# Dividing the normalization of the last row tile by columns among VectorE, ScalarE and GpSimd

## The reference

```python
def layer_norm(x, g, b):
    xf = x.astype(jnp.float32)
    mu = jnp.mean(xf, axis=-1, keepdims=True)
    var = jnp.mean(jnp.square(xf - mu), axis=-1, keepdims=True)
    return ((xf - mu) * lax.rsqrt(var + LN_EPS) * g + b).astype(x.dtype)
...
hp = layer_norm(ALPHA * hp + out_p, ln_g[l], ln_b[l])   # 16 meta rows are dropped later, 512 remain
hs = layer_norm(ALPHA * hs + out_s, ln_g[l], ln_b[l])   # 64 rows
```

## Time and profile before

| what | value |
|---|---|
| median of 3 runs | 1019.59 us (1019.33 to 1021.05) |
| the profiled execution's own time | 1020.12 us |
| its span, first to last instruction or landing | 1018.6 us |
| PE busy | 1000.1 us, 98% of the span |
| DVE busy | 715.8 us, 70% |
| ACT busy | 531.7 us, 52% |
| POOL busy | 79.0 us, 8% |
| end of the last matmul in the span | 1008.40 us |
| end of the last DVE instruction | 1015.70 us |

### The profile page before, as it was taken

One profiled execution on the slowest core, in us unless ns is written; L12 is line 12 of the kernel. 1 busy time (PEld: TensorE's weight loads), 2 busy tenths in 40 slices (PEclk: granted clock), 3 DMA queues, 4 the chain that ended last, 5 costly groups with the idle time before them and its releaser, 6 DMA issues.

```text
span 1018.6 us, 20283 instructions
## 1 busy us (share of the span) xinstructions
PE 1000.1 (98%) x7287; PEld 939.8 (92%) x7287; DVE 715.8 (70%) x1423; ACT 531.7 (52%) x1217; POOL 79.0 (8%) x156
## 2 busy tenths in 40 slices
PE   8999999999999999999999999999999999999995
PEld 6989999999999999999999999999999888888884
DVE  6988686876868677686867787767787655141685
ACT  6546455564645555464665776556677662111400
POOL 1520101001010010001010000000000000000000
PEclk9999999999999999999999999999999999999998
DMA  9142333232233313234321222231226543222423
GB/s 349 56 133 95 122 112 127 78 110 98 96 132 110 126 58 108 97 110 140 111 85 65 95 81 97 100 105 52 88 81 237 180 180 104 83 82 82 166 68 118
DMA packets 36258, 115.06 MB, mean 113 GB/s; under 512 B 9312, under 2 KB 9728, under 8 KB 33584
## 3 DMA queue, kind: packets, MB, share of 16 engines
q1 hardware_dynamic: 24208, 87.00, 24.8%
q0 software_dynamic: 11856, 27.14, 7.9%
q10 hardware_dynamic: 144, 0.26, 0.1%
HBM read 99.31 MB, written 18.29 MB: 115 GB/s over the span
## 4 chain that ended last, share of the span: by engine, by line
PE 95%; DMA 2%; DVE 1%; issue 1%; ACT 1%; SPq 0%; DVEq 0%; ACTq 0%
PE ps L1630 33%; PE ps L1640 27%; PE ps L1877 20%; PE ps L1842 5%; PE ps L1816 4%; PE ps L1800 2%; PE ps L1799 2%; DMA w_raw<-in_w_all 1%; PE ps L1862 1%; DMA pt<-in_w_ff 1%; PE ps L1721 1%; PE ps L1820 0%; DVE tb L1283 0%; DVE wl L1106 0%; DVE rows L1607 0%
## 5 line engine op out<-in xcount | busy, mean ns | idle before, releaser
L1630 PE MATMUL ps<-xh,wh 128*128 128x296 f32 (+1 forms) x864 | 261.3, 302 | 2.0 <-DMA pt<-in_w_ff 2.0
L1630 PE MATMUL ps<-xh,wl 128*128 128x296 f32 (+1 forms) x864 | 256.9, 297 | 0.0
L1630 PE MATMUL ps<-xl,wh 128*128 128x296 f32 (+1 forms) x864 | 256.8, 297 | 0.0
L1877 PE MATMUL ps<-wh,mix_parts 128*128 128x512 f32 x576 | 184.2, 390 | 0.0
L1630 PEld LDWEIGHTS ps<-xh,wh 128*128 128x128 f32 x864 | 163.4, 189 | 6.6 <-issue 2.9
L1630 PEld LDWEIGHTS ps<-xl,wh 128*128 128x128 f32 x864 | 163.7, 189 | 0.0
L1630 PEld LDWEIGHTS ps<-xh,wl 128*128 128x128 f32 x864 | 163.2, 189 | 0.0
L1106 DVE TENSOR_TENSOR wl<-w_raw,wh 128x1024 fp32r<-128x1024 f32 (+1 forms) x150 | 143.1, 954 | 19.5 <-ACT wh L841 8.1
L927 ACT ACTIVATE tb<-tb,small 128x256 f32<-128x256 f32 (+5 forms) x160 | 81.3, 508 | 93.4 <-DVE small L1302 64.8
L1877 PEld LDWEIGHTS ps<-wh,mix_parts 128*128 128x128 f32 x576 | 108.1, 188 | 22.4
L1877 PE MATMUL ps<-wl,mix_parts 128*128 128x512 f32 x320 | 124.5, 389 | 0.0
(11 more groups left out here) (196 smaller groups left out, 1732.0 us busy)
## 6 DMA issues: line engine op xcount, KB each, us to landing
w_raw<-in_w_all SPq DMA_DIRECT2D x106, 512.0 KB, 4.3
w_raw<-in_w_all SPq DMA_DIRECT2D x14, 1024.0 KB, 4.8
cbc<-c_rows POOLq DMA_DIRECT2D x16, 360.0 KB, 4.1
x_raw<-in_xT SPq DMA_DIRECT2D x7, 592.0 KB, 12.1
rows<-in_x_p POOLq DMA_DIRECT2D x4, 1024.0 KB, 5.3
out_y_p<-rows SPq DMA_DIRECT2D x16, 256.0 KB, 2.5
mix_rows<-mixT POOLq DMA_DIRECT2D x14, 288.0 KB, 2.4
rel_copies<-rel_rows POOLq DMA_DIRECT2D x8, 384.0 KB, 10.8
```

The source lines that it names most:

```text
L1630: ins = nc.tensor.matmul(ps[:, bank, result(tile, h)], a[f][:, w], b[:, ko, first:first + width], start=(ko == n_first and i == 0), stop=( ...
L1877: ins = nc.tensor.matmul(ps[:, bank, :], a, b[slot][:, w], start=(ko == 0 and i == 0), stop=(ko == KO - 1 and i == len(products) - 1))
```

## The change

Only the last row tile, m = 3, is treated differently. Its four quarters are divided by engine. Quarters 0 and 1 stay on DVE in the two passes of before. Quarter 2 (`mid`) is centred by DVE, scaled by rstd on ACT (`mid_scaled`), and gets its shift added on DVE, with a `tensor_tensor`. Quarter 3 (`end`) is centred and scaled in one ACT instruction, row * rstd + `offset`, where `offset` = -mean * rstd is a new [128, 1] value that DVE computes behind the reciprocal; then POOL multiplies it by gain and adds shift, in two `tensor_tensor` instructions with a wait between them. DVE's order in the last tile becomes: centre quarter 2, reciprocal, offset, centre quarters 0 and 1, scale quarters 0 and 1, add quarter 2's shift. SP stores quarters 0, 1 and 2 on `normed`, and quarter 3, last as before, on the new semaphore `pool_normed`. The other four row tiles keep their order. The diff, without the declarations of `offset` and of the six semaphores:

```diff
-NORM_CUTS = 4
+NORM_CUTS, DVE_CUTS = 4, 2
...
             for i, m in enumerate(last_order):
                 for j in range(NORM_CUTS):
                     c = norm_cut(j)
-                    sp.wait_ge(normed, NORM_CUTS * i + j + 1)
+                    if i == MT - 1 and j == NORM_CUTS - 1:
+                        sp.wait_ge(pool_normed, 1)
+                    else:
+                        sp.wait_ge(normed, NORM_CUTS * i + j + 1)
                     out = y_p[m * P:(m + 1) * P, c] if m < 4 else y_s[:, c]
                     sp.dma_start(out, rows[m][row_range(m), c]).then_inc(y_stored, 16)
             sp.wait_ge(y_stored, NORM_CUTS * 16 * MT)
...
             pool.dma_start(rows[3][:], x_p[3 * P:, :]).then_inc(rows_loaded[3], 16)
             pool.wait_ge(valued, 5 * PAIRS)
             pool.dma_start(rows[4][P - DEC_SEQ:, :], x_s).then_inc(rows_loaded[4], 16)
+            m, end = last_order[-1], norm_cut(NORM_CUTS - 1)
+            pool.wait_ge(norm_loaded, 32)
+            pool.wait_ge(end_scaled, 1)
+            nc.gpsimd.tensor_tensor(rows[m][:, end], rows[m][:, end], gain[:, end], ALU.mult).then_inc(end_gained, 1)
+            pool.wait_ge(end_gained, 1)
+            nc.gpsimd.tensor_tensor(rows[m][:, end], rows[m][:, end], shift[:, end], ALU.add).then_inc(pool_normed, 1)
             for s, n in ((v_stored, KV_SETS), (k_stored, KV_SETS), (kept_stored, 2), (lf_stored, 1)):
                 pool.wait_ge(s, 16 * n)
 
...
                 act.wait_ge(moments_ready, i + 1)
                 nc.scalar.activation(rstd[r, 0, m:m + 1], moments[r, m, 1:2], ACT.Sqrt,
                                      bias=eps[r, :]).then_inc(root_ready, 1)
+            m, mid, end = last_order[-1], norm_cut(DVE_CUTS), norm_cut(NORM_CUTS - 1)
+            act.wait_ge(offset_ready, 1)
+            nc.scalar.activation(rows[m][:, end], rows[m][:, end], ACT.Identity, scale=rstd[:, 1, m:m + 1],
+                                 bias=offset[:]).then_inc(end_scaled, 1)
+            act.wait_ge(mid_centred, 1)
+            nc.scalar.activation(rows[m][:, mid], rows[m][:, mid], ACT.Copy, scale=rstd[:, 1, m:m + 1]
+                                 ).then_inc(mid_scaled, 1)
 
 
 
...
                                   ).then_inc(moments_ready, 1)
                 dve.wait_ge(norm_loaded, 32)
                 dve.wait_ge(moments_ready, i + 1)
-                for j in range(NORM_CUTS):
-                    c = norm_cut(j)
-                    nc.vector.scalar_tensor_tensor(out=rows[m][r, c], in0=rows[m][r, c], scalar=moments[r, m, 0:1],
-                                                   in1=gain[r, c], op0=ALU.subtract,
-                                                   op1=ALU.mult).then_inc(centred, 1)
-                    if j == 0:
+                cuts = range(NORM_CUTS) if i < MT - 1 else range(DVE_CUTS)
+
+                def centre(c):
+                    return nc.vector.scalar_tensor_tensor(out=rows[m][r, c], in0=rows[m][r, c], scalar=moments[r, m, 0:1],
+                                                          in1=gain[r, c], op0=ALU.subtract, op1=ALU.mult)
+
+                if i == MT - 1:
+                    centre(norm_cut(DVE_CUTS)).then_inc(mid_centred, 1)
+                for j in cuts:
+                    if j == (1 if i < MT - 1 else 0):
                         dve.wait_ge(root_ready, i + 1)
                         nc.vector.reciprocal(rstd[r, 1, m:m + 1], rstd[r, 0, m:m + 1]).then_inc(rstd_ready, 1)
+                        if i == MT - 1:
+                            dve.wait_ge(rstd_ready, MT)
+                            nc.vector.scalar_tensor_tensor(out=offset[:], in0=moments[:, m, 0:1], scalar=-1.0,
+                                                           in1=rstd[:, 1, m:m + 1], op0=ALU.mult,
+                                                           op1=ALU.mult).then_inc(offset_ready, 1)
+                    centre(norm_cut(j)).then_inc(centred, 1)
                 dve.wait_ge(rstd_ready, i + 1)
-                for j in range(NORM_CUTS):
+                for j in cuts:
                     c = norm_cut(j)
                     dve.wait_ge(centred, NORM_CUTS * i + j + 1)
                     nc.vector.scalar_tensor_tensor(out=rows[m][r, c], in0=rows[m][r, c], scalar=rstd[r, 1, m:m + 1],
                                                    in1=shift[r, c], op0=ALU.mult, op1=ALU.add).then_inc(normed, 1)
+                if i == MT - 1:
+                    mid = norm_cut(DVE_CUTS)
+                    dve.wait_ge(mid_scaled, 1)
+                    nc.vector.tensor_tensor(rows[m][:, mid], rows[m][:, mid], shift[:, mid], ALU.add).then_inc(normed, 1)
 
 
 
```

More of the change, by code:

```diff
@@ L397, in build @@
         eps = sb("eps", [P, 1], F32, at=norm_at + 640)
+        offset = sb("offset", [P, 1], F32, at=norm_at + 672)
         sample_high = sb("sample_high", [P, 512], F32, at=norm_at + 704)
@@ L470, in build @@
         sample_joined, sample_added = sem("sample_joined"), sem("sample_added")
+        offset_ready, mid_centred, mid_scaled, end_scaled, end_gained, pool_normed = (
+            sem(n) for n in ("offset_ready", "mid_centred", "mid_scaled", "end_scaled", "end_gained", "pool_normed"))
         y_stored = sem("y_stored")
```

## The result

The changed kernel took 1021.81 us (median of 22 runs, 1020.06 to 1022.84), the kernel before 1019.50 us (22 runs, 1018.34 to 1021.29). The ratio is 1.0019 with a 95% interval of 1.0012 to 1.0025: about 1.9 us slower (the medians differ by 2.3). That is just inside the 0.2% that the prediction called no change, though the interval reaches past it, and 0.6 us more than its +1.3.

A forecast was written before the change was run, and what follows sets the result against it. PE bounds all but the tail, which is DVE's chain with transfers close behind; DVE's 1.17 us gain is outweighed by POOL's pair waiting its turn, so 1019.59 + 1.3 = 1020.9 us, range 1018.9 to 1022.0.

The forecast's parts named there:

- What leaves DVE: Tail behind the last matmul: with quarter work moved away, DVE alone ends 1.17 us earlier, at 1014.53.
- What ACT adds: Tail: ACT scales quarter 3 to about 1012.07, then quarter 2 to 1012.78, hidden with 1.06 us to spare.
- Theory B: Set for the follow-ups: new DVE-ACT waits cost the time; without POOL's part still about 1.5 us above, near 1021.
- The port: Tail from 1012.2: a POOL SBUF read and a two-input DVE instruction exclude each other; the loser waits it out.
- the two orders: Handover in the tail: DVE finishes first, +1.35 us, held likelier, or POOL and DVE alternate, +1.56 us.
- the prediction's two witnesses: Early POOL copies: one at 40.56 us waited through two overlapping DVE instructions; the 165-element one got in ahead of one.
- p: Time of one two-input POOL instruction on 128x512 in the tail: taken as 1.2 us, bounds 0.59 and 1.39.
- the in-turn sum: Tail with POOL and DVE instructions alternating: last store issued at 1017.30, landing at 1019.80, +1.56 us.
- rival 1: Tail: POOL runs beside DVE, ending at 1014.75; kernel 0.45 us earlier, 1019.1 us; chance 0.12.
- The signs of being wrong: Tail: POOL's addition ending before 1015.7, DVE waiting for `mid_scaled`, or first store after 1013.4 without POOL ahead.
- Rival 2's load: Before POOL's multiplication: a library's first call, some 6 us, last store near 1023.3, 5 us late; chance 0.02.
- the milder order: Tail: DVE finishes first at 1014.53, then POOL's pair; last store lands at 1019.59, +1.35 us.

The follow-up runs named there:

- the first experiment: The changed kernel with POOL's two instructions moved to DVE, behind quarter 2's last addition, ACT's part kept; 1.0005 (0.9996 to 1.0014) against the kernel before.

## Why the prediction was right, and where its sizes were off

- *What leaves DVE.* Right: 1.17 us. The kernel with shift in PSUM has DVE end 6.11 us behind the last matmul; the prediction's 1014.53 is 6.13 behind 1008.40.
- *What ACT adds.* Right, and hidden: 0.81 us for the scaling with two per-row operands (0.76 was taken), 0.71 for the other. Theory B, that the new waits cost the time, fell with the first experiment.
- *The port.* Right that POOL's reads and DVE's two-input instructions exclude each other: shown by taking the second input away (0.75 us again) and by adding POOL's pair alone (+2.0 us). Of the two orders, the one held to be less likely came: POOL gets in at the handover between two overlapping DVE instructions, each time, in all three kernels in which it meets instructions of two inputs (the changed one and those with POOL's pair and with its smaller one). Of the prediction's two witnesses the 165-element copy went the same way; why the one-element copy at 40.56 us waited through two instructions stays open.
- *p.* The sum took 1.2 us both as POOL's own time and as the time for which it holds DVE up. The hold is 1.0, the bound "two inputs one after the other" of 0.99. As a span in the profile a POOL instruction is longer (1.27 us with no two-input DVE instruction in its way, 1.45 and 1.59 with), so hold and span are two numbers. With 1.0 the in-turn sum puts the last issue at 8.5 us behind the matmul, which is the measured 8.54.
- *The stores.* Missed by 0.4 us: the sum in turn took a landing of 2.5 us. Three stores are issued within 1 us here, and the last lands after 2.9.
- *The end.* Missed by 0.4 us: the sum ended with the landing. POOL's drain was in no term, though its row stood in the trace before, at 841.3 us, 7.18 us long and hidden. Had the port been free (rival 1), the drain would have made that rival's gain a loss, as the kernel with shift in PSUM shows.
- *The signs of being wrong.* Two were set badly. POOL's addition ended at 1015.21, ahead of the 1015.7 that was to show the prediction wrong; but its own sum in turn has that end at 1015.58. And the last store, to be issued at 1017.1 or later, was issued at 1016.76, since p was too long. The first store came at 1014.12, later than 1013.4, with a POOL instruction ahead of it, as the text allowed.
- *Rival 2's load.* The prediction said that the order shows nothing that loads a library for POOL. It passed over the row `ISA` ahead of POOL's first instruction, which the trace has as a pair of MODIFY_POOL_CONFIG at 841.3 us. Whether they load anything is not shown; with 170 us of waiting behind them, their cost would be hidden. The kernel before has such a pair too, at 3.2 and 3.3 us, right ahead of its first select, which began at 3.33 us and took 287 ns: no cost shows there. From the view of the changed kernel's line:

```profile
L822 POOLq MODIFY_POOL_CONFIG  x2: 37/37/37, 841.3 to 841.4; - x2
```

In sum 1.2 (issue) + 0.4 (landing) + 0.4 (drain) is the measured 2.0 us of the tail; the forecast had 1.3, from a larger p and the milder order. The mechanism that decides, that POOL and DVE exclude each other, was foreseen. That the difference still stayed within 0.2% is in part luck: the sum in turn was too long by 0.4 us for p and too short by 0.8 us for the landing and the drain, and the ratio of 1.0019 lies at the edge, with an interval that leaves out 1. The kernel is slower, by little.

## What to carry to other kernels

Before work is moved from DVE to POOL, count the SBUF inputs of the DVE instructions beside it: those with two ran in turn with POOL's reads here, also with a POOL instruction of one input. Then weigh the hold against what leaves DVE: POOL held it for 1.0 us per instruction, and each instruction taken off it had cost some 0.6 us, so the move lost time even before the stores and the drain. In a tail, add what follows the last instruction of each engine, its drain and its stores, and not only the engine's work. A quarter taken off one engine shortens the tail only as far as the next chain, here the transfers, lets it.

## What the runs showed of the hardware that was not expected

- POOL's drain at the end of the program ends 5.0 to 5.2 us behind POOL's last instruction in five kernels, whether that is an addition of 512 columns, a copy or a memset of one column of 0.10 us. So POOL can end the program last although its work is done 2.7 us before the last store has landed, as in the kernel with shift in PSUM. DVE's drain is not like it: in the kernel with POOL's part moved to DVE it ends at 1014.9, as DVE's last addition does.
- PE's two fp32 products by a diagonal matrix took 1.98 us at full clock in the first of the two kernels that have them (0.9 each was expected): the granted clock was 1.00 (2.4 GHz) in its tail up to 1017 us, while in the kernel before, with PE idle behind its last matmul, it was 0.50 (1.2 GHz) from 1013 us on. Which of PE's products kept it up was not tried.
